# Two transformer blocks on one core: rotary partners from spare weight columns in both mixers, and a top-8 search in the second route

## The chip, the core and the metric

The kernel is written for Trainium2 and runs on one NeuronCore of it. The core has a matrix engine (TensorE, PE in the profile, with its weight loads shown apart as PEld), a vector engine (VectorE, DVE), an activation engine (ScalarE, ACT), GpSimd (POOL) and a queue that issues DMAs (SyncE, SP). Each runs its own list of instructions; they wait for one another through semaphores. The metric is device time in microseconds. The kernel before took 2412.55 us (median of three runs, 2411.41 to 2412.77).

## What is computed

256 tokens of width 1024 pass through a first block of two layers and a second block of one, all in float32. A layer of the first block is a mixer and a feed-forward part: the first layer's is dense, the second layer's is a mixture of 8 experts with 2 chosen per token. The second block is a hybrid layer (a recurrence and a dilated attention), and then a mixture of 32 experts in 4 groups. The parts that matter here, cut from the reference:

```python
def rope(x, positions):                       # in both mixers of the first block
    ...
    x1, x2 = xf[..., :half], xf[..., half:]   # half = 16
    return jnp.concatenate([x1 * cos - x2 * sin, x1 * sin + x2 * cos], axis=-1)

q = (rms_norm(c_q, q_norm_g) @ w_uq).reshape(B, S, MLA_HEADS, MLA_NOPE + MLA_ROPE)   # 8 heads, 64 + 32
q_rope = rope(q[..., MLA_NOPE:], positions)
k_rope = rope(k_r[:, :, None, :], positions)[:, :, 0, :]

# route of the second block's mixture
grp_logits = h @ w_router_group + b_router_group                  # 4 groups
grp = jnp.argmax(grp_logits, axis=-1)
exp_logits = (h @ w_router_expert + b_router_expert).reshape(N, 4, 8)[tok_idx, grp]
top_v, top_i = lax.top_k(exp_logits, 2)
gate = grp_p * jax.nn.softmax(top_v, axis=-1)
```

## The kernel before, in words

**Layout.** Activations lie with channels on the 128 partitions and the 256 tokens in the free dimension (`x_chan`, `h_chan`: 8 tiles of 128x256). Constants of the program lie in one table, `tab_sb` (`TAB`, L47), a 128-row array of 128-column parts such as `ident`, `ones`, `iota` and `rot1`; the queue loads it in the setup between the fourth and the fifth of its weight loads (L363). Weights come from DRAM as a stream of 1 MB slots into a ring of 14 slots, `ring`, by DMAs that SP issues (L138); a slot is loaded again when its user has counted it as used.

**Order of the stages** (L3347 to L3363): setup, mixer 0, dense, mixer 1, first mixture, hybrid, second mixture. Each stage is made of blocks, and every engine waits at the end of a block for the others (the profile shows that as a wait for PEq).

**A mixer's first block** (`stage_mixer`, L546) makes 34 products, listed in `items`: tiles of the input projection (n = 0 to 7), one query product per head (n = 8 to 15, L639), one key product per head, two value products, and eight more tiles of the input projection (n = 26 to 33, L631 and L634). The banks of PSUM go round in fives, and ACT copies each product out. The query product gives 96 rows: 64 plain ones and, on partitions 64 to 95, the 32 that are rotated. The spare part of the weight slot, 32 more columns per head, holds zeros.

**The rotation before.** `turn(i)` (L657) is called on PE behind products 27 to 31. For i < 4 it multiplies the rows 64 to 95 of two heads (32x512) by a 32x32 matrix, `rot1`, that swaps the two halves and negates one; for i = 4 the same for the shared key (32x256). The product goes to one of two PSUM banks (`rot_banks`). DVE waits for it (`rot_done`), multiplies it by the sines (L771), the rows themselves by the cosines (L772) and adds both (L773); for the key L779 to L781. In mixer 0 DVE also computes parts of the modulation vector from side loads of 1 MB (`dve_modulation`, L324), three of them between the rotations. A side load goes out when a slot of its own ring of four is free.

**A mixer's other blocks**: causal attention (L898 and on), and the output projection (L812). At the start of the latter SP begins to load the next stage's weights (`nxt.head`).

**The second route** (`TokenRoute`, L1306) comes before the second mixture. ACT, PE and DVE turn the router's product into 36 logits per token (2 tiles of tokens on 128 partitions). Then DVE works through one instruction after another, each waiting for the one before (`link`): `first_max` (L1292) on the 4 groups; the group's choice is spread over its 8 experts by a product of the choice with itself (L1379); the experts outside the group are pushed down to -1e30 (L1380 to L1382); `first_max` for the best expert with 7 instructions and for the second best with 6; and the sum of both choices (L1385). PE, which has run 10 products only to keep busy (L314), waits for that sum, counts the places (L1350, L1352), DVE makes the selection (L2015), PE gathers the tokens of the first experts (L2047), and the experts' products (L2063, L2086) follow. The ring then has 20 slots, filled before the route ends.

Of the kernel before, what the change touches and what calls it, by code (L numbers as in the profile page):

```python
# [14 lines left out]
P = 128  # L15
# [31 lines left out]
def table_columns():  # L47

    cols = [("ident", 128), ("ones", 128), ("heads2", 128), ("tri", 128), ("rot1", 128), ("rot2", 128),
            ("freq1", 1), ("freq2", 1), ("causal", 128), ("iota", 128), ("eps", 1), ("row", 1)]  # L50
    at, out = 0, {}
    for name, n in cols:
        out[name] = slice(at, at + n)
        at += n
    return out, at
# [490 lines left out]
def stage_mixer(k, l, loads, nxt, norm, nxt_norm, side=None):  # L546
# [4 lines left out]
    with ExitStack() as ctx:  # L551
# [20 lines left out]
        banks, rot_banks, lat_sums = k.bank[1:6], k.bank[6:8], k.bank[0]  # L572
# [11 lines left out]
        rot_done, rope_ready = S("rot_done"), S("rope_ready")  # L584
        forget_step, forget_moved = S("forget_step"), S("forget_moved")
        with nc.Block() as block:
# [31 lines left out]
            def _(pe):  # L618
                def product(n):
# [16 lines left out]
                    elif kind == "query":  # L636
                        w = w.rearrange("p (t h m) -> p t h m", t=2, h=HEADS)
                        for t in range(2):
                            mm = nc.tensor.matmul(b[0:96, 0:T], w[:, t, i, 0:96], cq[:, t, :], start=(t == 0),  # L639
                                                  stop=(t == 1))  # L640
# [16 lines left out]
                def turn(i):  # L657
                    pe.wait_ge(*tile_out.at(10 + 2 * i if i < 4 else 4))
                    if i >= 2:
                        pe.wait_ge(*rope_ready.at(i - 1))  # L660
                    src = qm[64:96, 2 * i:2 * i + 2, :] if i < 4 else misc[64:96, :]
                    nc.tensor.matmul(rot_banks[i % 2][64:96, 0:512 if i < 4 else T], k.t("rot1")[64:96, 64:96], src,
                                     start=True, stop=True).then_inc(*rot_done.up())

                keep_warm(k, k.bank[7], 10 if l else 5)
                for n in range(len(items)):
# [7 lines left out]
                    if 27 <= n < 32:  # L674
                        turn(n - 27)

            @block.scalar
            def _(act):
# [7 lines left out]
                for n, (kind, j, i) in enumerate(items):  # L686
                    act.wait_ge(*item_done(n))
                    b = banks[n % NB]
                    if kind == "query":
                        a(qm[0:96, i, :], b[0:96, 0:T], ACT.Copy, scale=96 ** -0.5).then_inc(*tile_out.up())  # L690
# [31 lines left out]
            def _(dve):  # L722
# [41 lines left out]
                for i in range(5):  # L764
                    dve.wait_ge(*rot_done.at(i + 1))
                    b = rot_banks[i % 2]
                    if i < 4:
                        swapped = b[64:96, :].rearrange("p (h n) -> p h n", h=2)
                        x = qm[64:96, 2 * i:2 * i + 2, :]
                        turned = scratch[64:96, 3:5, :]  # L770
                        link(v.tensor_tensor(turned, swapped, spread(sin[64:96, :], 2), ALU.mult))  # L771
                        link(v.tensor_tensor(x, x, spread(cos[64:96, :], 2), ALU.mult))  # L772
                        v.tensor_tensor(x, x, turned, ALU.add).then_inc(*rope_ready.up())  # L773
                        dve.wait_ge(*rope_ready.last())
# [2807 lines left out]
```

## Time and profile before

| what | us |
|---|---|
| median of three runs | 2412.55 |
| the profiled execution | 2411.62 |
| its span, from the first to the last instruction | 2409.8 |
| setup | 0 to 34.8 |
| mixer 0 | 35 to 181 |
| dense | 181 to 477 |
| mixer 1 | 477 to 628 |
| first mixture and hybrid | 628 to 1952 |
| route of the second mixture | 1952 to 1962 |
| second mixture | 1962 to 2409.8 |

The page of the profile gives PE busy for 92% of the span, DVE for 29%, ACT for 13%, and 734.71 MB moved at a mean of 305 GB/s. Its second part cuts the span into 40 slices and gives for each the busy tenths of every engine, the clock granted to TensorE and the DMA rate; its fourth part follows the chain of work that ended last. From the trace come tables of the instructions in order of time, grouped tables with the mean of one instruction (ns), tables of who waited for whom, and tables of stretches with the busy time of each engine, the granted clock and the DMA rate. In the order-of-time tables a value in brackets is the idle time of the engine before the instruction and what ended it.

### The profile page before, as it was taken

The numbers are of one execution on the slowest core, as the hardware profiler recorded it, in microseconds if no ns is written. First come the engines' busy times: TensorE is split into PE (matmuls) and PEld (weight loads), VectorE is DVE, ScalarE is ACT, GpSimd is POOL, SyncE is SP. The second block draws the span as 40 slices with busy tenths as digits, with TensorE's granted clock in tenths as the row PEclk, the third lists the DMA queues.
The fourth block names the chain that finished last, engine by engine and source line by source line (L and its number), as shares of the span: only waits on it lengthen the run. The fifth ranks groups of instructions, "written<-read, shape, count | busy, mean of one in ns | idle before, by whom it ended". The sixth has DMA issues, their size and how long they took to land. (4 is left out here: it accounts for less than half of the span.)

```text
span 2409.8 us, 47351 instructions
## 1 busy us (share of the span) xinstructions
PE 2223.1 (92%) x21866; PEld 1356.5 (56%) x21866; DVE 689.6 (29%) x1274; ACT 319.3 (13%) x717; POOL 23.2 (1%) x21
## 2 busy tenths in 40 slices
PE   6999999999999999999999999899999997777776
PEld 5778888877734344353534444688789862221221
DVE  6763222336501101101101102455465431111111
ACT  2331000144200000000000000333232110000000
POOL 1000000000000000000000000000000000000000
PEclk9999999999999999999999999999999998877778
DMA  9658555701699999999999999433300579999998
GB/s 398 244 231 336 213 225 209 322 12 60 254 397 407 408 401 419 398 420 401 420 392 420 394 419 417 176 123 140 128 3 4 217 296 421 421 421 422 421 421 365
DMA packets 111472, 734.71 MB, mean 305 GB/s; under 512 B 12768, under 2 KB 16128, under 8 KB 36640
## 3 DMA queue, kind: packets, MB, share of 16 engines
q1 hardware_dynamic: 109328, 724.62, 74.2%
q8 instruction: 176, 2.88, 0.5%
q0 software_dynamic: 1152, 4.19, 0.4%
q10 hardware_dynamic: 784, 2.75, 0.3%
q14 instruction: 32, 0.26, 0.0%
HBM read 721.39 MB, written 10.09 MB: 304 GB/s over the span
## 5 line engine op out<-in xcount | busy, mean ns | idle before, releaser
L1558 PE MATMUL bank<-ring,moe_xg 128*32 128x512 f32 (+1 forms) x6144 | 581.0, 540 | 0.7 <-DVE moe_xg L1714 0.7
L1558 PEld LDWEIGHTS bank<-ring,moe_xg 128*32 128x32 f32 x6144 | 199.1, 110 | 377.3 <-issue 375.3
L1569 PE MATMUL bank<-ring,moe_turned 128*32 128x256 f32 x5376 | 291.5, 379 | 0.0
L1569 PEld LDWEIGHTS bank<-ring,moe_turned 128*32 128x32 f32 x5376 | 174.7, 110 | 117.1 <-issue 3.1
L1117 PE MATMUL bank<-h_chan,ring 128*128 128x256 f32 x896 | 195.6, 379 | 1.4 <-ACT h_chan L503 1.4
L1117 PEld LDWEIGHTS bank<-h_chan,ring 128*128 128x128 f32 x896 | 170.2, 190 | 24.7 <-issue 1.6
L2063 PE MATMUL bank<-ring,late 128*32 128x512 f32 x696 | 122.9, 806 | 51.8 <-DMA ring<-stream 51.8
L1753 DVE TENSOR_TENSOR moe_hidden<-moe_silu,bank 128x512 f32<-128x512 f32 (+1 forms) x48 | 26.9, 617 | 482.9 <-PE bank L1558 482.9
L2508 PE MATMUL bank<-h_chan,ring 128*128 128x256 f32 x672 | 148.0, 380 | 1.9 <-DVE h_chan L2613 1.9
L2508 PEld LDWEIGHTS bank<-h_chan,ring 128*128 128x128 f32 x672 | 127.0, 190 | 23.0 <-issue 6.3
L2063 PEld LDWEIGHTS bank<-ring,late 128*32 128x32 f32 x696 | 17.7, 122 | 150.2 <-DMA ring<-stream 129.8
L1101 PE MATMUL bank<-dense_hidden,ring 128*128 128x256 f32 x448 | 98.8, 379 | 0.0
L1707 DVE COPY moe_y<-bank 32x256 f32<-32x256 f32 x48 | 20.0, 416 | 257.1 <-PE bank L1569 256.5
L1101 PEld LDWEIGHTS bank<-dense_hidden,ring 128*128 128x128 f32 x448 | 85.1, 190 | 11.6
L631 PE MATMUL bank<-h_chan,ring 128*128 128x256 f32 x384 | 85.1, 380 | 1.0 <-ACT h_chan L503 1.0
L2086 PE MATMUL bank<-ring,moe_turned 128*32 128x512 f32 x392 | 58.7, 704 | 27.6 <-DMA ring<-stream 26.8
L631 PEld LDWEIGHTS bank<-h_chan,ring 128*128 128x128 f32 x384 | 72.5, 190 | 15.0 <-issue 5.5
L1615 ACT ACTIVATE moe_silu<-bank 128x512 f32<-128x512 f32 (+1 forms) x48 | 22.6, 544 | 434.6 <-PE bank L1558 434.6
L2129 DVE TENSOR_TENSOR moe_hidden<-late,bank 128x512 f32<-128x512 f32 x8 | 5.5, 687 | 240.2 <-PE bank L2063 240.2
L324 DVE CUSTOM_DVE_ANT_0 ada_product<-ada_slots,ada_c 128x1024 f32<-128x1024 f32 x56 | 68.5, 1223 | 1.5
L1134 DVE TENSOR_TENSOR dense_hidden<-dense_silu,bank 128x512 f32<-128x512 f32 x14 | 9.6, 688 | 201.3 <-PE bank L1117 201.3
L1698 ACT ACTIVATE moe_y<-bank 32x256 f32<-32x256 f32 x48 | 18.1, 377 | 354.2 <-PE bank L1569 353.8
(461 smaller groups left out, 2119.2 us busy)
## 6 DMA issues: line engine op xcount, KB each, us to landing
ring<-stream SPq DMA_DIRECT2D x257, 1024.0 KB, 22.7
ring<-wide SPq DMA_DIRECT2D x240, 1024.0 KB, 16.8
ring<-wide SPq DMA_DIRECT2D x128, 768.0 KB, 16.9
late<-stream SPq DMA_DIRECT2D x47, 1024.0 KB, 27.0
ada_slots<-stream SPq DMA_DIRECT2D x28, 1024.0 KB, 7.2
h_chan<-stream SPq DMA_DIRECT2D x9, 1024.0 KB, 26.7
rows<-zeros SPq DMA_DIRECT2D x8, 512.0 KB
moe_x_rows<-rows SPq DMA_DIRECT2D x28, 96.0 KB, 10.8
```

The source lines that it names most:

```text
L324: mul = k.nc.vector.tensor_tensor_reduce(product, w[:, i * D:(i + 1) * D], c_row, 1.0, 0.0, ALU.mult, ALU.add, accum_out=k.mod[:, l, at:at ...
L631: mm = nc.tensor.matmul(b[:, 0:T], w[:, t, i * P:(i + 1) * P], k.hT[:, t, :], start=(t == 0), stop=(t == DT - 1))
L1101: mm = nc.tensor.matmul(k.bank[t // 2][:, (t % 2) * T:(t % 2) * T + T], w[:, f, t * P:(t + 1) * P], hidden[:, c % 2, f, :], start=(c == 0 ...
L1117: mm = nc.tensor.matmul(b[:, f * T:(f + 1) * T], w[:, t, f * P:(f + 1) * P], k.hT[:, t, :], start=(t == 0), stop=(t == DT - 1))
L1558: mm = self.k.nc.tensor.matmul(banks[r][i * TILE:(i + 1) * TILE, 0:width], self.m.xg[:, r, t * TILE:(t + 1) * TILE], w[:, i, :], start=(t ...
L1569: mm = self.k.nc.tensor.matmul(self.sum_bank[r][q * TILE:(q + 1) * TILE, :], self.m.turned[:, r, n * TILE:(n + 1) * TILE], w[:, f2, q * T: ...
L1615: k.nc.scalar.activation(m.silu[:, r, 0:self.span[c]], self.gate_bank[r][:, 0:self.span[c]], ACT.Silu)\
L1707: last = self.k.nc.vector.tensor_copy(self.m.y[r * TILE:(r + 1) * TILE, q * T:(q + 1) * T], self.sum_bank[r][q * TILE:(q + 1) * TILE, :])
L1753: v.tensor_tensor(m.hidden[:, r, 0:self.span[c]], m.silu[:, r, 0:self.span[c]], self.up_bank[r][:, 0:self.span[c]], ALU.mult).then_inc(*se ...
L2063: mm = k.nc.tensor.matmul((self.gate_bank if j < self.per_proj else self.up_bank)[own, :], m.xg[:, t, own], w[:, i, e, :], start=(t == 0), ...
L2086: mm = k.nc.tensor.matmul(k.bank[half][own, :], m.turned[:, f, own], w[:, i, e, :], start=(f == 0), stop=(f == 3))
L2508: mm = nc.tensor.matmul(b[:, 0:T], lhsT, rhs, start=(t == 0), stop=(t == DT - 1))
```

## The change

It has two parts. In the mixers, the weights' 32 spare columns per query head, and 32 columns of the tile `misc` that holds the shared key, now hold the 32 rotary columns with their halves swapped; so the same product yields the swapped rows on partitions 96 to 127. ACT copies 128 rows instead of 96. The sines on those partitions are taken from a frequency column whose first half is negated. The products with `rot1`, their two semaphores and the table part `rot1` go. DVE takes the swapped rows from SBUF.

In the second route, the mask of the group is added to the logits directly, and both calls of `first_max` on the experts are replaced by `max` (the eight largest values of each row) and `max_index` (their positions), one of each per tile of tokens, a copy that turns positions into float32, and two comparisons with `iota`.

```diff
-    cols = [("ident", 128), ("ones", 128), ("heads2", 128), ("tri", 128), ("rot1", 128), ("rot2", 128),
+    cols = [("ident", 128), ("ones", 128), ("heads2", 128), ("tri", 128), ("rot2", 128),
...
-                            mm = nc.tensor.matmul(b[0:96, 0:T], w[:, t, i, 0:96], cq[:, t, :], start=(t == 0),
-                                                  stop=(t == 1))
+                            mm = nc.tensor.matmul(b[:, 0:T], w[:, t, i, :], cq[:, t, :], start=(t == 0), stop=(t == 1))
...
-                def turn(i):
-                    pe.wait_ge(*tile_out.at(10 + 2 * i if i < 4 else 4))
-                    if i >= 2:
-                        pe.wait_ge(*rope_ready.at(i - 1))
-                    src = qm[64:96, 2 * i:2 * i + 2, :] if i < 4 else misc[64:96, :]
-                    nc.tensor.matmul(rot_banks[i % 2][64:96, 0:512 if i < 4 else T], k.t("rot1")[64:96, 64:96], src,
-                                     start=True, stop=True).then_inc(*rot_done.up())
...
-                    if 27 <= n < 32:
-                        turn(n - 27)
...
-                        a(qm[0:96, i, :], b[0:96, 0:T], ACT.Copy, scale=96 ** -0.5).then_inc(*tile_out.up())
+                        a(qm[:, i, :], b[:, 0:T], ACT.Copy, scale=96 ** -0.5).then_inc(*tile_out.up())
...
-                    dve.wait_ge(*rot_done.at(i + 1))
-                    b = rot_banks[i % 2]
                     if i < 4:
-                        swapped = b[64:96, :].rearrange("p (h n) -> p h n", h=2)
-                        x = qm[64:96, 2 * i:2 * i + 2, :]
+                        dve.wait_ge(*tile_out.at(10 + 2 * i))
+                        swapped, x = (qm[rows, 2 * i:2 * i + 2, :] for rows in (slice(96, 128), slice(64, 96)))
                         turned = scratch[64:96, 3:5, :]
-                        link(v.tensor_tensor(turned, swapped, spread(sin[64:96, :], 2), ALU.mult))
+                        link(v.tensor_tensor(turned, swapped, spread(sin[96:128, :], 2), ALU.mult))
                         link(v.tensor_tensor(x, x, spread(cos[64:96, :], 2), ALU.mult))
-                        v.tensor_tensor(x, x, turned, ALU.add).then_inc(*rope_ready.up())
-                        dve.wait_ge(*rope_ready.last())
+                        link(v.tensor_tensor(x, x, turned, ALU.add))
...
+        link(v.tensor_scalar(col["ghot"], col["ghot"], -NEG, NEG, ALU.mult, ALU.add))
         for tok in range(TT):
-            own = spread_last(m.small["ghot"][:, tok, :], E // G)
-            link(v.tensor_tensor(m.small["hot1"][:, tok, :].rearrange("p (g e) -> p g e", g=G), own, own, ALU.mult))
-        link(v.tensor_tensor(L, L, hot1, ALU.mult))
-        link(v.tensor_scalar(hot1, hot1, -NEG, NEG, ALU.mult, ALU.add))
-        link(v.tensor_tensor(L, L, hot1, ALU.add))
-        first_max(k, m, link, L, E, col["m1"], hot1, col["l2"])
-        first_max(k, m, link, col["l2"], E, col["m2"], hot2, None)
+            own = m.small["l"][:, tok, :].rearrange("p (g e) -> p g e", g=G)
+            link(v.tensor_tensor(own, own, spread_last(m.small["ghot"][:, tok, :], E // G), ALU.add))
+        for tok in range(TT):
+            link(v.max(m.best[:, tok, :], L[:, tok, :]))
+        for tok in range(TT):
+            link(v.max_index(m.best_at[:, tok, :], m.best[:, tok, :], L[:, tok, :]))
+        link(v.tensor_copy(m.best_place[:, :, :], m.best_at[:, :, 0:2]))
+        iota = spread(k.t("iota")[:, 0:E], TT)
+        for i, hot in enumerate((hot1, hot2)):
+            link(v.tensor_tensor(hot, iota, m.best_place[:, :, i:i + 1].broadcast_to([P, TT, E]), ALU.is_equal))
+        col["m1"], col["m2"] = m.best[:, :, 0:1], m.best[:, :, 1:2]
...
+    t[96:128, TAB["freq1"].start] = np.concatenate([-f1, f1])
...
+        misc[:, 96:112], misc[:, 112:128] = kr[:, 16:32], kr[:, 0:16]
...
+        uq[:, :, :, 96:112], uq[:, :, :, 112:128] = uq[:, :, :, 80:96], uq[:, :, :, 64:80]
```

## Rows read from the trace of the kernel before

**Rows 1.** The page: span in 40 slices, in tenths, and GB/s.
```profile
PE   6999999999999999999999999899999997777776
...
PEclk9999999999999999999999999999999998877778
DMA  9658555701699999999999999433300579999998
```
**Rows 2.** Who PE waited for, from 1960 us on: us, times, longest.
```profile
PE bank L2063 <- DMA ring<-stream: 51.8, 60, 2.2
PE bank L2086 <- DMA ring<-stream: 26.8, 26, 1.4
```
**Rows 3.** Stretches: length, PE, PEld, DVE, ACT, POOL busy; clock, DMA share, GB/s.
```profile
180.00:475.00 295.00, 293.28 (x1368) 258.26 (x1369) 86.64 (x148) 17.94 (x32) 0.96 (x1) 1.00 0.64 258
...
655.00:1590.00 935.00, 927.30 (x11789) 421.56 (x11782) 122.97 (x253) 71.15 (x161) 3.79 (x4) 1.00 0.96 384
...
1970.00:2400.00 430.00, 316.28 (x1900) 97.11 (x1892) 57.94 (x105) 7.86 (x16) 0.00 (x0) 0.79 1.01 420
```
**Rows 4.** Order of time, PE, end of mixer 0's first block.
```profile
85.63 1.04 PE L662 MATMUL bank<-qm,tab_sb 32*32 32x512 f32 x2
...
90.25 1.04 PE L662 MATMUL bank<-qm,tab_sb 32*32 32x512 f32 x2
...
104.66 7.17 PE L634 MATMUL bank<-ring,h_chan 128*128 128x256 f32 x32
112.56 0.67 PE L898 MATMUL bank<-km,qm 96*128 96x256 f32 x2 [0.73 <-PEq L586]
```
**Rows 5.** Order of time, DVE, mixer 0.
```profile
83.94 0.08 DVE L324 DVE_READ_ACCUMULATOR2_ANT mod<- 128x1 f32 x1
...
86.81 0.69 DVE L771 TENSOR_TENSOR score<-bank,sin 32x512 f32<-32x512 f32 x1 [2.79 <-PE bank L662]
...
88.97 1.23 DVE L324 CUSTOM_DVE_ANT_0 pT<-ring,score 128x1024 f32<-128x1024 f32 x1
...
91.50 0.69 DVE L771 TENSOR_TENSOR score<-bank,sin 32x512 f32<-32x512 f32 x1
...
104.84 0.42 DVE L779 TENSOR_TENSOR score<-bank,sin 32x256 f32<-32x256 f32 x1 [1.83 <-PE bank L662]
...
108.26 0.17 DVE L344 SCALAR_TENSOR_TENSOR amp<-mod,vec_sb 128x8 f32<-128x8 f32 x1
```
**Rows 6.** Stretches of mixer 0 with the side loads' DMA at the end of each row.
```profile
80.00:85.00 5.00, 5.00 (x25) 4.41 (x24) 3.91 (x8) 0.76 (x2) 0.00 (x0) 1.00 1.01 416
85.00:90.00 5.00, 5.00 (x22) 3.36 (x20) 3.09 (x4) 0.76 (x2) 0.00 (x0) 1.00 0.69 282
```
**Rows 7.** Order of time, mixer 1: PE's first and last rotation, DVE's wait.
```profile
532.16 1.04 PE L662 MATMUL bank<-qm,tab_sb 32*32 32x512 f32 x2
...
533.31 0.69 DVE L771 TENSOR_TENSOR score<-bank,sin 32x512 f32<-32x512 f32 x1 [15.37 <-PE bank L662]
...
551.19 7.17 PE L634 MATMUL bank<-ring,h_chan 128*128 128x256 f32 x32
```
**Rows 8.** Tile `ring`, 60 to 110 us: duration min/median/max in ns, first and last start.
```profile
L631 PEld LDWEIGHTS bank<-h_chan,ring x89: 186/190/190, 59.9 to 94.3; 128*128 128x128 f32 x89
...
L639 PEld LDWEIGHTS bank<-pT,ring x32: 160/163/163, 65.3 to 72.7; 128*96 128x96 f32 x32
```
**Rows 9.** Order of time: twenty of the query's matmuls on PE; copies of 96 and 128 rows.
```profile
49.13 0.40 ACT L698 ACTIVATE pT<-bank 128x256 f32<-128x256 f32 x1
...
65.51 4.48 PE L639 MATMUL bank<-pT,ring 128*96 128x256 f32 x20
...
71.59 0.38 ACT L690 ACTIVATE qm<-bank 96x256 f32<-96x256 f32 x1 [0.17 <-PE bank L639]
```
**Rows 10.** Order of time, setup: DVE's wait for a weight load.
```profile
22.49 1.23 DVE L324 CUSTOM_DVE_ANT_0 h_chan<-ring,h_chan 128x1024 f32<-128x1024 f32 x1 [3.60 <-DMA ring<-stream]
```
**Rows 11.** Order of time, second route: DVE's chain, and PE around it.
```profile
1954.75 0.17 DVE L1298 TENSOR_SCALAR moe_idx<-moe_ghot 128x8 f32<-128x8 f32 x1
...
1954.96 0.17 DVE L1299 TENSOR_TENSOR moe_idx<-moe_idx,tab_sb 128x8 f32<-128x8 f32 x1
...
1955.76 0.42 DVE L1379 TENSOR_TENSOR moe_hot<-moe_ghot 128x32 f32<-128x32 f32 x2
1956.21 0.23 DVE L1380 TENSOR_TENSOR moe_l<-moe_l,moe_hot 128x64 f32<-128x64 f32 x1
...
1956.96 0.22 DVE L1296 TENSOR_REDUCE moe_m<-moe_l 128x2 f32<-128x64 f32 x1
1957.21 0.22 DVE L1297 TENSOR_TENSOR moe_hot<-moe_l,moe_m 128x64 f32<-128x64 f32 x1
...
1960.25 0.23 DVE L1385 TENSOR_TENSOR moe_chosen<-moe_hot 128x64 f32<-128x64 f32 x1
...
1960.53 0.43 PE L1350 MATMUL bank<-moe_chosen,tab_sb 128*128 128x64 f32 x2 [3.23 <-DVE moe_chosen L1385]
```
**Rows 12.** Order of time: both gathers on PE, and SP's first load after the route.
```profile
1962.17 5.44 PE L2047 MATMUL bank<-moe_pick,late 128*128 128x128 f32 x32 [0.56 <-DVE moe_pick L2015]
...
1968.66 6.34 SPq L138 DMA_DIRECT2D ring<-stream  x8
...
1981.68 1.95 PE L2047 MATMUL bank<-moe_pick,late 128*128 128x128 f32 x16
```
**Rows 13.** Stretches around the falls of the clock, second route and mixer 0.
```profile
139.80:143.20 3.40, 3.40 (x18) 2.96 (x14) 1.28 (x4) 0.62 (x2) 0.00 (x0) 0.53 0.00 0
...
1962.20:1965.70 3.50, 3.50 (x17) 3.50 (x18) 0.11 (x1) 0.09 (x1) 0.00 (x0) 0.52 0.00 0
```
**Rows 14.** Order of time, PE in mixer 0's attention, ahead of its fall of the clock.
```profile
138.71 0.66 PE L911 MATMUL bank<-tab_sb,score 128*128 128x128 f32 x4 [1.68 <-DVE score L1004]
...
140.09 2.50 PE L314 MATMUL bank<-tab_sb 128*128 128x128 f32 x10
...
144.94 1.16 PE L314 MATMUL bank<-tab_sb 128*128 128x128 f32 x8
```
**Rows 15.** The chain that ended last: its end and one turn of the stream.
```profile
2373.53 27.82 DMA ring<-stream
...
2401.40 1.11 PE bank L2086 x8
```

More of the change, by code:

```diff
@@ L571, in stage_mixer @@
         z, lo, e, F, negF = (scratch[0:8, i, :] for i in (3, 4, 5, 6, 7))
-        banks, rot_banks, lat_sums = k.bank[1:6], k.bank[6:8], k.bank[0]
+        banks, lat_sums = k.bank[1:6], k.bank[0]
         NB = len(banks)
@@ L583, in stage_mixer @@
         lat_root, lat_ready = S("lat_root"), S("lat_ready")
-        rot_done, rope_ready = S("rot_done"), S("rope_ready")
         forget_step, forget_moved = S("forget_step"), S("forget_moved")
@@ L778, in _ @@
                         turned, own = scratch[64:96, 3, :], scratch[64:96, 4, :]
-                        link(v.tensor_tensor(turned, b[64:96, 0:T], sin[64:96, :], ALU.mult))
+                        link(v.tensor_tensor(turned, misc[96:128, :], sin[96:128, :], ALU.mult))
                         link(v.tensor_tensor(own, misc[64:96, :], cos[64:96, :], ALU.mult))
@@ L2288, in __init__ @@
         self.mark = sb("mark", [1, 8])
+        self.best, self.best_place = sb("best", [P, TT, 8]), sb("best_place", [P, TT, 2])
+        self.best_at = sb("best_at", [P, TT, 8], mybir.dt.uint32)
         self.inverse = sb("inverse", [P, TT])
@@ L3431, in tables @@
     t[:, TAB["tri"]] = (p[:, None] <= p[None, :])
-    rot1 = np.zeros((P, P), np.float32)
-    for i in range(16):
-        rot1[64 + 16 + i, 64 + i] = -1
-        rot1[64 + i, 64 + 16 + i] = 1
-    t[:, TAB["rot1"]] = rot1
     rot2 = np.zeros((P, P), np.float32)
```

## The prediction, made before the changed kernel ran

> **What bounds the kernel now.** I read the page's slices first [rows 1]. PE is at nine tenths until the last eight slices, where it drops to seven and the DMA row stands at nine: the kernel has a long part bound by PE and a last part bound by the weight stream. The stretches say the same [rows 3]: in the dense stage PE is busy for 293.28 of 295 us with the DMA engines at a 0.64 share; in the first mixture 927.30 of 935 us; from 1970 us on PE has 316.28 of 430 us while the DMA moves 420 GB/s without a gap. There PE's waits are for loads [rows 2], and the chain that ended last is DMA to its end [rows 15]. So the reader has to ask two things of an edit: does it shorten what PE does before 1952 us, and does it bring forward the moment at which the last stream restarts? That stream fills its 20 slots before the route ends, stands still, and restarts at 1968.66 when the first slot has been used [rows 12]. From there to the end all is bytes divided by rate. Every stream before it starts at a block's beginning or when PE or DVE gives a slot back; none starts by a time of its own. Hence a stage that ends d earlier moves all behind it by d, whether that part is bound by PE or by DMA.
>
> **Mixers: what goes.** The rotation is five pairs of PE matmuls per mixer between the last products. In mixer 0 the first begins at 85.63 and the last product group, two products long, at 104.66 [rows 4]. That is 19.03 us for four products and five rotations. Two products without a rotation between them take 7.17 us [rows 4], so one takes 3.585, four take 14.34, and the rotations cost 19.03 - 14.34 = **4.69 us** on PE. (One cycle: 90.25 - 85.63 = 4.62, less 3.585, is 1.035 for a 512-wide rotation with its gaps.) Mixer 1 shows 532.16 to 551.19, again 19.03 [rows 7], again 4.69. PE sets the end of the block in both: it waits for nothing until the block's end at 112.56 (0.73 for the others) [rows 4]. Sum: **-9.38 us**.
>
> **What is late next.** In mixer 0 DVE ends at 108.43 and PE at 111.83 [rows 4, 5]. If PE ended at 107.14 and DVE stayed, DVE would keep 1.3 of the 4.69. But DVE too starts earlier: it idled 2.79 us for the first rotation and 1.83 for the last [rows 5], and now needs only the rows of ACT's query copies, which run around 71.6 us [rows 9]. From 83.94 on it has four rotations of 2.16 (86.81 to 88.97), three modulation steps of 2.53 (88.97 to 91.50) and 3.59 for the key and the tail (104.84 to 108.43) [rows 5]: 83.94 + 0.1 + 8.64 + 7.59 + 3.59 = 103.9, which is 3.3 us ahead of PE's new end. The modulation steps need side loads; the DMA falls to a 0.69 share in 85 to 90 us, so its queue is empty at about 88.5 [rows 6], and the last two steps now begin at 90.9 and 95.6. The first would begin at 86.2, with its load three behind the queue's end (2.4 us each at 416 GB/s: 81). Cost: nothing. If that cover were gone, each microsecond of lateness beyond 3.3 would count fully. In mixer 1 DVE waited 15.37 us [rows 7]; all its rotation will be done before PE's last two products start.
>
> **What is added there.** Query weights grow from 96 to 128 columns, which lie in slots that are loaded anyway. A weight load takes 163 ns for 96 columns and 190 for 128 [rows 8]. But twenty query matmuls end in 4.48 us, 0.224 each [rows 9], and products with 128 columns run at the same 3.585/16 = 0.224 [rows 4]: the 256-column stream sets the pace, and the load hides under it. ACT's copy takes 0.38 for 96 rows and 0.40 for 128 [rows 9]. Both at zero; above, 32 loads x 27 ns = 0.86 us per mixer if the load were bare; below zero nothing, since no work goes. The page "TensorE: Matmul & The Clock Gate" of the Trainium skill (Step-by-step: what each phase is for) says that a weight load's time scales with the column count, and the two durations agree with it. Taken as a rule for the time of the products it would speak against this change, and the sum would be 1.7 us higher; the equal pace of the products says it does not reach the path. DVE now multiplies from SBUF instead of PSUM, off the path.
>
> **Setup.** The table shrinks by 128 columns, 65.5 KB. It lies in the queue before the weight load for which DVE waits 3.60 us [rows 10], and DVE sets the setup's end. At 420 GB/s [rows 3] that is **-0.16 us**.
>
> **Second route.** From 1955.76, the first L1379, to 1960.25, the sum of the choices, DVE runs 18 linked instructions in 4.49 us [rows 11], with PE waiting (3.23 us of idle time ends at L1385). All 18 go. In their place, by start-to-start distances: a scalar op on 128x8, 0.21 (1954.75 to 1954.96); two additions on 128x32, 0.45 for both (the two L1379); a copy of 128x4, 0.21 as well; two comparisons on 128x64, 0.26 each, 0.52. That is 1.39. The four search instructions have no row. One takes at least what a tiny op takes, 0.21, and `max` most likely what a reduction on 128x64 takes, 0.25 (1956.96 to 1957.21) [rows 11]. `max_index` reads two inputs and writes eight positions; I bound it by one tiny op below (0.21) and three full ones above (0.76), and take 0.40, in the middle of one and two full ones, since both its inputs are short. So 0.50 + 0.80 = 1.30; bounds 4 x 0.21 = 0.84, and with two full ones for a `max` 2 x 0.51 + 2 x 0.76 = 2.54. New chain 1.39 + 1.30 = 2.69: **-1.80 us** (bounds -2.26 and -0.56). The Trainium skill's "Vector Engine (DVE) Microarchitecture Reference" (The match/index hardware and the swap-based sort pattern) says that finding positions is a separate pass of two instructions, a load of the eight values and a search. By it each `max_index` would be 0.21 + 0.25 = 0.46 and the gain 1.68; no row here shows it.
>
> **The clock behind the route.** PE's granted clock is 0.52 (1.2 GHz for nearly all of it) from 1962.2 to 1965.7 [rows 13], behind the idle 3.23 us and a further 0.56 [rows 11, 12]. The gather of 32 matmuls runs in it and takes 5.44 us, where 16 take 1.95 at full clock [rows 12], 3.90 for 32: the fall costs 1.54. The new wait is 3.23 - 1.80 = 1.43. Nearest rows: in mixer 0 a wait of 1.68 with shorter stops around it is followed by a fall at 139.8 [rows 13, 14], and at 112.56 a stop of 0.73 is not: the slices stay at nine tenths there [rows 1, 4]. 1.43 lies between, nearer the first, but the keep-busy matmuls run right up to it. I take the full clock: **-1.54 us**, the least certain term; bound on the other side 0.
>
> **Sum** against the profiled execution: 2411.62 - 0.16 - 9.38 - 1.80 - 1.54 = 2398.7. The median lay 0.93 above that execution, so **2399.7**.
>
> **Rivals.** (a) The clock still falls behind the shorter wait: 2401.2. For it: 1.68 was enough in the mixer. (b) The search instructions are slow: at 0.78 us each on average (3.10 for the four) the route gains nothing and the clock falls as before, 2403.0. Against: no DVE instruction on so few elements in the chain takes over 0.26. (c) The falls in the mixers' attention move or vanish, as everything behind the first block shifts. There ten keep-busy matmuls took 2.50 us and eight took 1.16 at full clock [rows 14], so about 1.05, and with what follows 1.3 per mixer: 2397.1 with both gone; a new one in another place would cost as much. (d) The mixers' gain is taken back in part by a side load or DVE in mixer 0 that is late by over 3.3 us: up to 4.69 back, 2404.4. (e) Slower: with the table shorter by 512 bytes per partition, every tensor behind it lies at another address. If the stream wrote more slowly there, the last part alone, 432.7 us from 1968.66 to 2401.36 [rows 12, 15], would give back 12.9 us at a rate 3% lower (408 instead of 420 GB/s), and from there on the kernel is slower; at 4% it is 2417. For it speaks only that the last part has no slack at all; against it that very different targets (ring, late, h_chan) now all run at that rate. (f) The change does nothing that shows, because what the rotations cost sits in some wait I misread: 2412.
>
> **Chances.** Forecast 0.46, (a) 0.22, (b) 0.09, (c) 0.11, (d) 0.06, (e) 0.04, (f) 0.02. The range 2396.0 to 2404.5 takes in the forecast, (a), (b), (c), most of (d), and the bounds of the search. A measurement of this kernel can tell about 0.2% (4.8 us) from no change: faster 0.93, same 0.03, slower 0.04.
>
> **What would show it.** Each mixer's last tiles of products would follow one another at 3.585 us without L662, and attention begin 4.85 us earlier in mixer 0 and 9.5 earlier in mixer 1 (both with setup's 0.16). The route from its first instruction to the sum of the choices would be 1.80 shorter, the gather near 3.9 us with a clock of 1.00, and SP's first load after it about 13 us earlier than 1968.66. From there to the end nothing should differ by over a microsecond. I would be wrong if DVE's end replaced PE's in mixer 0, if a search instruction took over 0.5 us, or if the stream's rate moved.

## The result

| | median, us | lowest and highest | runs |
|---|---|---|---|
| before | 2412.66 | 2411.41 to 2412.94 | 4 |
| changed | 2394.76 | 2391.22 to 2396.21 | 4 |

The ratio is 0.9923 [0.9911, 0.9936]: 17.9 us faster, where 12.9 were forecast. The sign was right and the time lies 1.2 us below the range. The profiled execution took 2391.22, the fastest of the four, so its trace shows more gain (20.4 us) than the median does. With the runs of the experiments, before has 51 runs from 2406.6 to 2415.5 with a median of 2411.8, and the changed kernel 15 from 2391.2 to 2396.7 with a median of 2395.0: 16.8 us apart. The first three runs of before lay closer together than the kernel's runs do. Of the ten runs with the rotations put back (ghost_turns), one took 3306.92 us at a granted clock of 0.65 and is left out of what follows.

**The page of the changed kernel**, PE, granted clock and DMA in 40 slices:

```profile
span 2389.4 us, 47297 instructions
...
PE   6999999999999999999999999899999997777776
...
PEclk9999999999999999999999999999999998787777
DMA  9668554802699999999999999343300579999998
```

Against [rows 1] it is the same picture, shorter: a long part at nine tenths of PE, then eight slices in which the DMA row stands high.

**Mixers.** PE in order of time, mixer 0: the last 64 matmuls of one line of products, the 64 of the other, and the first of the attention.

```profile
78.47 13.98 PE L630 MATMUL bank<-h_chan,ring 128*128 128x256 f32 x64
92.29 13.98 PE L633 MATMUL bank<-ring,h_chan 128*128 128x256 f32 x64
106.99 1.32 PE L883 MATMUL bank<-km,qm 96*128 96x256 f32 x5 [0.73 <-PEq L585]
```

The eight products follow one another with nothing between. From 78.47 to 92.29 four take 13.82 us, so 3.455 each. The attention starts at 106.99, against 112.56 in [rows 4]. DVE in the same stretch, its first rotation and its last instruction, and then its first and last step of the rotation in mixer 1:

```profile
83.87 0.69 DVE L757 TENSOR_TENSOR score<-qm,sin 32x512 f32<-32x512 f32 x1
...
103.52 0.17 DVE L344 SCALAR_TENSOR_TENSOR amp<-mod,vec_sb 128x8 f32<-128x8 f32 x1
...
510.80 0.69 DVE L757 TENSOR_TENSOR score<-qm,sin 32x512 f32<-32x512 f32 x1
...
520.33 2.28 DVE L766 TENSOR_TENSOR km<-score 32x2048 f32<-32x2048 f32 x1
```

DVE no longer waits in its rotation ([rows 5] had 2.79 and 1.83) and ends at 103.7, 2.6 us ahead of PE's last product (92.29 + 13.98 = 106.27) and 3.3 ahead of its next block. From SBUF the multiplication takes 0.69, as from PSUM.

**Second route.** DVE from the group's choice to the chosen experts, then PE, then SP's first load:

```profile
1938.41 0.17 DVE L1362 TENSOR_SCALAR moe_ghot<-moe_ghot 128x8 f32<-128x8 f32 x1
...
1939.07 0.42 DVE L1367 MAX8 moe_best<-moe_l 128x8 f32<-128x32 f32 x2
...
1939.53 0.09 DVE L1369 MATCH_VALUE_LOAD moe_best_at<-moe_best,moe_l 128x8 f32 x1
1939.61 0.18 DVE L1369 FIND_INDEX8 moe_best_at<-moe_best,moe_l 128x8 uint32<-128x32 f32 x1
...
1940.12 0.17 DVE L1370 CAST moe_best_place<-moe_best_at 128x4 f32<-128x4 uint32 x1
...
1940.85 0.22 DVE L1375 TENSOR_TENSOR moe_chosen<-moe_hot 128x64 f32<-128x64 f32 x1
...
1941.12 0.43 PE L1335 MATMUL bank<-moe_chosen,tab_sb 128*128 128x64 f32 x2 [1.18 <-DVE moe_chosen L1375]
...
1942.77 3.81 PE L2037 MATMUL bank<-moe_pick,late 128*128 128x128 f32 x32 [0.56 <-DVE moe_pick L2005]
...
1947.63 2.04 SPq L138 DMA_DIRECT2D ring<-stream  x3
```

The four searches, from 1939.07 to the copy at 1940.12, take 1.05 us. PE waits 1.18 instead of 3.23 [rows 11], the gather takes 3.81 instead of 5.44 [rows 12], and the first load goes out at 1947.63 instead of 1968.66, 21.03 earlier. In the three later profiles of the changed kernel it goes out at 1951.69, 1949.69 and 1952.38.

**To the end** the chain is DMA, as in [rows 15]:

```profile
2352.58 27.91 DMA ring<-stream
2380.53 1.11 PE bank L2076 x8
```

From SP's first load to the end of the last DMA it is 432.9 us; it was 432.7. All that was gained by 1947 us arrives at the end, less 0.2 in the stream and 0.5 in the tail.

**The account of the two profiled executions**, from landmarks of the order of time (us). A stage starts with SP's first small load (`posi` for the mixers and the hybrid), attention ends where the output projection's first matmul starts, and the tokens of the first mixture are SP's reads `moe_x_rows` for its first and its last expert.

| stretch | before | changed | difference |
|---|---|---|---|
| mixer 0, start to attention | 77.28 | 71.90 | -5.38 |
| mixer 0, attention | 33.83 | 32.24 | -1.59 |
| mixer 1, start to attention | 79.55 | 74.16 | -5.39 |
| mixer 1, attention | 33.50 | 32.24 | -1.26 |
| mixer 1, output projection to the first tokens of the first mixture | 74.79 | 74.47 | -0.32 |
| last tokens of the first mixture to the hybrid | 224.33 | 221.13 | -3.20 |
| hybrid to the router | 350.82 | 350.81 | -0.01 |
| group's choice to chosen experts | 4.69 | 2.64 | -2.05 |
| first gather | 5.36 | 3.74 | -1.62 |
| last DMA to the end | 8.45 | 8.91 | +0.46 |

The dense stage is 297.7 in both. The mixers' first blocks, the choice and the gather make 14.4 us; attention and the first mixture's end another 6. Is that second part due to the change?

### The profile page after: what moved, and what is told of

It reads as the page before. It is cut to its first block and busy times, and to the rows that moved or that the text cites. A ratio compares the mean times of both kernels' runs of the same rounds, so it can differ in the third digit from the quotient of the medians.

```text
span 2389.4 us, 47297 instructions
## 1 busy us (share of the span) xinstructions
PE 2206.5 (92%) x21846; PEld 1351.1 (57%) x21846; DVE 687.8 (29%) x1268; ACT 319.3 (13%) x717; POOL 23.3 (1%) x21
## 5 line engine op out<-in xcount | busy, mean ns | idle before, releaser
L1086 PEld LDWEIGHTS bank<-dense_hidden,ring 128*128 128x128 f32 x448 | 85.1, 190 | 11.6
L2053 PE MATMUL bank<-late 128*32 128x512 f32 x280 | 47.7, 782 | 21.7 <-DMA late<-stream 21.7
```

The source lines that it names most:

```text
L1086: mm = nc.tensor.matmul(k.bank[t // 2][:, (t % 2) * T:(t % 2) * T + T], w[:, f, t * P:(t + 1) * P], hidden[:, c % 2, f, :], start=(c == 0 ...
L2053: mm = k.nc.tensor.matmul((self.gate_bank if j < self.per_proj else self.up_bank)[own, :], m.xg[:, t, own], w[:, i, e, :], start=(t == 0), ...
```

## Experiments

Three questions. **First**, whether the mixers' 10.8 us are the time of the rotations on PE, or come with what else the change moved (a shorter table, addresses, an earlier DVE). **Second**, whether the gather's clock hangs on the length of the wait ahead of it. **Third**, whether the gain in attention belongs to the change; the theory is that waits of PE bring a lower clock and that filling them gains time, its rival that the falls come and go by themselves and the median doesn't show them. A keep-busy call (`keep_warm`) is one float32 matmul in the program and two in the trace. The kernel before took 2412.0 beside after_again and the kernels with one part alone or before_warm, 2411.6 beside after_look, ghost_turns, slow_route and after_warm2, and 2412.3 beside the rest.

### The same kernel again

No edit. after_again and after_b are five runs each, after_look is one.

> The changed kernel once more, for a profile of another execution. Theory: what does not depend on the clock is fixed at -13.0 us (setup 0.19, two mixer fronts 5.38 and 5.40, route 2.05), and the rest, up to 7.9 us in the first profile, is PE time at the lower clock level, which differs from execution to execution; so the time lies anywhere between 2390 and 2399, and the stage lengths outside stretches of the lower clock repeat within 0.1 us. Rival: everything in the first profile repeats, and the time is 2391 to 2392 each time.

Measured: 2395.17 (2394.49 to 2396.68), 0.9927 [0.9914, 0.9941].

> One more execution of the changed kernel. Both theories: fronts 71.90 and 74.17, route 2.64 from the group's comparison to the sum of the choices, gather 3.8 or 5.4. Theory (the lower clock comes and goes by execution): another set of stretches at 1.2 GHz than in the two profiles so far, and stage lengths that differ only there.

Measured: 2392.8, one run.

> The changed kernel once more, beside the next kernel on the same chip. All theories: 2393 to 2396 median. In 6 of the 7 profiles so far in which the 1.68 us wait was left as it is, each attention took 33.3 to 33.8 us, in the first profile of the changed kernel 32.24; so here too 33.3 to 33.8 in at least one of them.

Measured: 2394.94 (2393.93 to 2395.89), 0.9929 [0.9916, 0.9942]. (after_again's mixer 1, at 32.24, is overlooked in the count of the expectation.)

The first blocks of the mixers, the choice and the gather repeat to 0.01 us in all four profiles (these three and the first). Attention doesn't. In after_again, after_look and after_b it took 33.72, 33.30 and 33.79 in mixer 0 and 32.24, 33.57 and 32.23 in mixer 1. The stretch 132 to 135 us (columns: length, PE, PEld, DVE, ACT, POOL busy; clock, DMA share, GB/s), the changed kernel's first profile and then after_again's:

```profile
132.00:135.00 3.00, 1.85 (x18) 1.52 (x19) 2.41 (x9) 2.54 (x11) 0.00 (x0) 1.00 0.00 0
```

```profile
132.00:135.00 3.00, 2.02 (x12) 1.44 (x12) 2.28 (x7) 2.65 (x11) 0.00 (x0) 0.64 0.00 0
```

PE of the second in order of time:

```profile
132.98 1.12 PE L896 MATMUL bank<-tab_sb,score 128*128 128x128 f32 x4 [1.69 <-DVE score L989]
...
135.07 1.94 PE L314 MATMUL bank<-tab_sb 128*128 128x128 f32 x10
```

Two executions of one program, with the same wait of 1.69, and only one fell. So the 2.85 us in attention are luck of the profiled execution. The end of the first mixture came out at 222.36, 221.12 and 222.41. The 224.33 of before is no fixed cost of the kernel before either: route_only, which has the same mixture and the old mixers, took 220.45.

The lower clock accounts for the differences among these executions. From the first mixer to the end of the gather, the granted clock was at its lower level for 10.2 us in the changed kernel's first profile and for 20.5, 17.1 and 20.5 in the three repeats; in the profile of before it was 23.9. after_again's 10.2 us more cost it 4.2 us from mixer 0's start to SP's first load: 1.5 in mixer 0's attention, 1.5 at the start and 1.2 at the end of the first mixture, with all other rows of the table equal to 0.1.

### One part alone

mixers_only has the change's hunks of the table and of `stage_mixer` with their weights; the route stays as before.

```diff
-                def turn(i):
...
-                        turn(n - 27)
```

> The kernel before with the mixers' part of the change alone. Theory: setup and two fronts, 0.19 + 5.38 + 5.40 = 10.97, and up to 5 us of falls of the clock in the attentions and at the end of the first mixture: 2397 to 2402. The second route keeps its 3.2 us wait and its slow gather of about 5.4 us. Rival (the forecast's own term, 4.69 per mixer, and the rest of the gain sits in the route): 2403 with no more than 9.6 before the second route.

Measured: 2400.39 (2397.57 to 2403.58), 0.9947 [0.9934, 0.9961]: -11.6. The first blocks take 71.90 and 74.17, as in the changed kernel, and the choice 4.69, as before.

```profile
92.44 13.98 PE L633 MATMUL bank<-ring,h_chan 128*128 128x256 f32 x64
107.14 3.69 PE L883 MATMUL bank<-km,qm 96*128 96x256 f32 x16 [0.73 <-PEq L585]
...
1949.77 0.43 PE L1335 MATMUL bank<-moe_chosen,tab_sb 128*128 128x64 f32 x2 [3.24 <-DVE moe_chosen L1370]
1951.41 6.67 PE L2032 MATMUL bank<-moe_pick,late 128*128 128x128 f32 x32 [0.45 <-DVE moe_pick L2000]
```

route_only has the hunks of `TokenRoute.dve` and its tiles; the mixers stay as before.

```diff
-        first_max(k, m, link, L, E, col["m1"], hot1, col["l2"])
-        first_max(k, m, link, col["l2"], E, col["m2"], hot2, None)
...
+            link(v.max(m.best[:, tok, :], L[:, tok, :]))
...
+            link(v.max_index(m.best_at[:, tok, :], m.best[:, tok, :], L[:, tok, :]))
```

> The kernel before with the route's part alone. Theory: the chain from the group's mask to the sum of the choices is 2.05 us shorter, the gather runs at full clock (3.81 instead of 5.44 us) behind a wait of 1.2 us, in all -3.7: 2409.0; if the clock falls behind the shorter wait too, -2.1: 2410.6. All before the route is as before. Rival (the search also pays an entry cost or the route was hidden by the stream): 2412 to 2413.

Measured: 2408.02 (2405.18 to 2413.22), 0.9979 [0.9970, 0.9988]: -4.0. The first blocks take 77.28 and 79.54 and the choice 2.64. The profiled execution was the slowest of the eleven.

```profile
1960.32 0.43 PE L1350 MATMUL bank<-moe_chosen,tab_sb 128*128 128x64 f32 x2 [1.19 <-DVE moe_chosen L1390]
...
1962.09 5.44 PE L2052 MATMUL bank<-moe_pick,late 128*128 128x128 f32 x32 [0.70 <-DVE moe_pick L2020]
```

The parts add up to -15.6, beside -16.8 for the whole; within the intervals nothing says that they touch one another. And here the gather is slow behind a wait of 1.19: the short wait doesn't exclude the fall (rival (a)), it only makes it rarer.

### The rotations put back as empty work

The changed kernel with the table's old length and five matmuls of the old shapes at the old places, whose product nobody reads or waits for:

```diff
+                def turn(i):
+                    src = k.tab[64:96, 0:512 if i < 4 else T]
+                    nc.tensor.matmul(k.bank[6 + i % 2][64:96, 0:512 if i < 4 else T], k.t("ident")[64:96, 64:96], src,
+                                     start=True, stop=True)
...
+                    if 27 <= n < 32:
+                        turn(n - 27)
```

> The changed kernel with the five rotation products of each mixer put back on PE where they stood, on constants of the table, nobody waiting for them; rot1 is back in the table; all else as in the changed kernel. Theory: the products cost PE 5.38 us per mixer by themselves, so the distance from a mixer's first DMA to its attention is 77.28 and 79.55 us again, and the time is some 10.8 above the changed kernel, about 2405 to 2407. Rival: part of the gain came from DVE's waits or from the sines and rows in SBUF; then the distances come out below 77.2 and 79.5.

Measured: 2407.77 (2403.10 to 2410.25, nine runs), 0.9984 [0.9974, 0.9993]. The first blocks take 77.32 and 79.58 us again, as before (77.28 and 79.55), while DVE does its rotation as early as in the changed kernel:

```profile
85.36 1.04 PE L657 MATMUL bank<-tab_sb 32*32 32x512 f32 x2
86.33 3.72 PE L630 MATMUL bank<-h_chan,ring 128*128 128x256 f32 x16
89.98 1.04 PE L657 MATMUL bank<-tab_sb 32*32 32x512 f32 x2
...
112.29 1.97 PE L890 MATMUL bank<-km,qm 96*128 96x256 f32 x8 [0.73 <-PEq L585]
```

```profile
83.74 0.69 DVE L764 TENSOR_TENSOR score<-qm,sin 32x512 f32<-32x512 f32 x1
```

That settles the first question: the mixers' 10.8 us are PE's own time for these five rotations, and DVE's wait took no part. The rows also part the cost of one (two matmuls in the trace): 0.97 from the start of a rotation to the product behind it, and 3.65 from that product to the next rotation, where 16 matmuls among their like take 3.455. So a rotation of 512 columns costs 0.97 for itself and 0.19 around it, and the one of 256 columns 0.54 (104.12 to 104.66 in the profile of before) and the same around it: 4 x 1.16 + 0.73 = 5.4 per mixer, all of the difference. The old addresses came back in this run together with the rotations, so the run alone doesn't part the two. The rows do: the products run at the same distance of 0.216 with the old addresses and with the new.

The median tells less. It lies 12.8 above the changed kernel's 2395.0, where the expectation had 10.8 and 2405 to 2407. These further 2.0 us don't stand in the first blocks.

### The wait ahead of the gather, made long again

The changed kernel with eight linked DVE instructions whose result isn't used, ahead of the new route's `col["m1"], col["m2"]`; timed twice.

```diff
+ for _ in range(8):
+     link(v.tensor_tensor(m.small["idx"][:, :, :], hot1, hot1, ALU.mult))
```

> The changed kernel with eight more linked DVE instructions of 128x64 in the route ahead of the sum of the choices, which PE waits for: 8 x 0.256 = 2.05 us. Theory A (a longer wait of PE brings the lower clock): wait 3.2 us, the gather takes 5.4 instead of 3.8 us, +3.7 in all. Theory B (a wait of 3.2 us and one of 1.2 us differ little, whether the clock falls there is chance): chain +2.05 and the gather 3.8 or 5.4. In both the chain from the group's mask to the sum of choices is 4.69 and nothing before it moves.

Measured: 2400.76 (2398.22 to 2402.50), 0.9957 [0.9942, 0.9972].

> The kernel with eight more linked DVE instructions in the route, again, beside the changed kernel on one chip, since four runs could not tell 3.7 from 5.9 us. Theory A (the longer wait brings the lower clock nearly every time): gather 5.2 to 6.6 us, median 3.5 to 4.0 above the changed kernel's. Theory B (a matter of chance either way): gather 3.8 or 5.4, median 2.0 to 2.9 above.

Measured: 2400.06 (2398.93 to 2402.53), 0.9951 [0.9938, 0.9964], 5.1 above the changed kernel beside it.

```profile
1946.28 2.04 DVE L1375 TENSOR_TENSOR moe_idx<-moe_hot 128x64 f32<-128x64 f32 x8
...
1948.64 0.43 PE L1335 MATMUL bank<-moe_chosen,tab_sb 128*128 128x64 f32 x2 [3.26 <-DVE moe_chosen L1377]
...
1950.28 5.39 PE L2039 MATMUL bank<-moe_pick,late 128*128 128x128 f32 x32 [0.56 <-DVE moe_pick L2007]
```

The delay is 2.07 us, the wait is back at 3.26 and the gather at 5.39: 3.6 us together. Gathers behind a wait of 3.2 were slow in 4 of 4 profiles (before, mixers_only and these two), behind one of 1.2 with the same ten keep-busy matmuls in 1 of 6. So the gather's clock does hang on the wait ahead of it, as theory A has it, with a chance and not a certainty. The median, 5.1 above, lies outside both theories (3.5 to 4.0, and 2.0 to 2.9), and some 1.5 of it stay unexplained. In the profiles one more fall, in mixer 1's attention (33.82 against after_b's 32.23), makes 1.6; whether the other executions had it is not known.

### Filling the waits

On the kernel before: keep-busy matmuls behind the last but one unit of each attention, more of them in the route, and some at the end of the first mixture.

```diff
+ if u == N - 2:
+     keep_warm(k, k.bank[5], 6)          # causal_attention
...
- keep_warm(k, k.bank[5], 10)             # TokenRoute.pe
+ keep_warm(k, k.bank[5], 22)
...
+ keep_warm(k, k.bank[0], 14)             # ahead of the wait for y_ready
```

> The kernel before, unchanged but for keep-busy matmuls on PE in four places where it waited: 6 in each mixer's attention ahead of the 1.68 us wait, 14 ahead of the wait at the end of the first mixture, 22 instead of 10 in the second route ahead of the 3.23 us wait. Theory (the falls follow PE's waits): the falls at 139.8, 586.9, 1528.9 and 1962.2 go, 1.4 + 1.3 + 1.5 + 1.6 = about 5.8 us: 2407. Rival (the falls come from something else, and the matmuls are only added work): 2412.7, or up to 1 us more.

Measured: 2412.14 (2408.55 to 2415.23), 0.9998 [0.9989, 1.0007]. The median did not move, though both attentions took 32.24. The other fillers did not do what they were put there for. First the route, then the end of the first mixture:

```profile
1957.05 5.52 PE L314 MATMUL bank<-tab_sb 128*128 128x128 f32 x44
...
1963.94 3.81 PE L2050 MATMUL bank<-moe_pick,late 128*128 128x128 f32 x32 [0.56 <-DVE moe_pick L2018]
```

```profile
1526.88 5.49 PE L314 MATMUL bank<-tab_sb 128*128 128x128 f32 x28 [4.80 <-issue]
```

In the route the clock fell ahead of the fillers, at 1954.6, where it had not fallen in the profile of before. The 22 calls (44 matmuls) started late and in part at the lower clock (granted 0.91 over 1957.0 to 1962.6). They held the gather at 3.81 but ended past the choice, and cost 0.83 between the choice and the gather. At the end of the mixture the stop of PE, 4.80 us, stands ahead of the 14 calls (28 matmuls) and is no wait for what comes behind them. They could not fill it; the clock fell within it, at 1524.5, and they ran 5.49 us at a granted 0.58. The stretch took 225.84. So this place was not tested. The same on the changed kernel, shorter, and without it:

```diff
+ if u == N - 2:
+     keep_warm(k, k.bank[5], 6)
...
- keep_warm(k, k.bank[5], 10)
+ keep_warm(k, k.bank[5], 14)
```

> The changed kernel with 6 keep-busy matmuls ahead of the 1.68 us wait in both attentions, and 14 instead of 10 in the second route; nothing is added at the end of the first mixture. Theory A (the falls follow PE's waits): both attentions take 32.24 us and the gather 3.8 in every execution, the median falls by 1 to 2 us to about 2393. Theory B (stretches of the lower clock come elsewhere instead): 2394 to 2396, as the changed kernel.

Measured: 2394.81 (2391.21 to 2397.04), 0.9935 [0.9921, 0.9948].

> The changed kernel with 6 keep-busy matmuls in both attentions and 14 in the second route, again, now beside the changed kernel on one chip. Theory A (filling the wait takes the fall away and nothing comes in its place): both attentions 32.2, and the median 2 to 3 us below the changed kernel's beside it. Theory B (what is won there comes back as other stretches of the lower clock): attentions 32.2 all the same, medians within 1 us.

Measured: 2393.85 (2391.72 to 2399.50), 0.9923 [0.9911, 0.9936]. The profile of after_warm2_b around the filled wait of mixer 0, as a stretch and on PE:

```profile
132.00:135.00 3.00, 2.86 (x27) 2.33 (x27) 2.41 (x8) 2.54 (x11) 0.00 (x0) 1.00 0.02 5
```

```profile
131.51 1.60 PE L314 MATMUL bank<-tab_sb 128*128 128x128 f32 x12
...
134.44 1.38 PE L314 MATMUL bank<-tab_sb 128*128 128x128 f32 x10
```

Filled, attention takes 32.2 us in 8 of 8 cases (four profiles, two mixers); unfilled it took 33.3 to 33.8 in 9 of 10 profiles in mixer 0 and in 7 of 10 in mixer 1. So the wait does bring the fall. Yet ten runs of this version have a mean of 2394.6, and the 15 without the filler one of 2394.7. In the profiled execution of after_warm2_b the clock was low twice in the hybrid:

```profile
1532.50:1537.50 5.00, 5.00 (x17) 4.08 (x17) 4.76 (x17) 0.01 (x1) 0.00 (x0) 0.66 0.86 347
...
1809.00:1814.00 5.00, 4.82 (x112) 4.68 (x108) 1.86 (x3) 1.19 (x2) 0.00 (x0) 0.66 0.00 0
```

PE is busy in these stretches, but it had stopped ahead of each:

```profile
1532.02 8.18 PE L2502 MATMUL bank<-h_chan,ring 128*128 128x256 f32 x29 [1.88 <-DVE h_chan L2607]
...
1808.28 1.15 PE L3067 MATMUL bank<-ring,late 64*64 64x64 f32 x32 [1.58 <-DVE ring L3272]
```

The clock fell at 1533.4 and at 1809.9, 1.4 and 1.6 us behind these stops. The stretch from the hybrid to the router took 354.5, and 350.8 in most others. That need not be the price of the filling: route_only's profile, with nothing filled, fell at the same two places (354.4). All 14 profiles have the stop of 1.88 and only three fell behind it, two of the four filled ones and one of the ten others. With eight more calls at the end of the first mixture:

```diff
+ keep_warm(k, k.bank[0], 8)              # ahead of the wait for y_ready
```

> As after_warm2_b, and 8 keep-busy matmuls (2.0 us at full clock, 3.9 at the lower) ahead of the wait of 3.8 us at the end of the first mixture. Theory A: the distance from the last read of the first mixture's rows to the hybrid stage is 220.4 to 221.2 us, as in the profiles with the shortest one, 1 to 2 us below the usual; median 1 us below after_warm2_b. Theory B: the lower clock there does not come from that wait, the distance stays between 221 and 223.

Measured: 2396.29 (2391.89 to 2401.35), 0.9935 [0.9921, 0.9948]. The end of the mixture took 223.72, longer than in the changed kernel's four profiles (221.12 to 222.41), and a low stretch stands in the hybrid again. Here too the stop stands ahead of the fillers:

```profile
1514.11 3.79 PE L314 MATMUL bank<-tab_sb 128*128 128x128 f32 x16 [3.37 <-issue]
```

No version came out clearly ahead of the changed kernel. So the third question has two answers. The waits in attention bring the falls there (16 of 20 unfilled, 0 of 8 filled), as the theory says; that filling them shortens the median is not shown.

## Why the forecast was right, and where it was not

**What bounds the kernel**: right. A stage that ends earlier moved all behind it; the last stream kept its length (432.5 to 432.9 us in all 14 profiles), so rival (e) fell with its price of 12.9 us.

**Mixers, what goes**: the mechanism was right, the term was too small. Forecast 4.69 per mixer, measured 5.38, with 1.39 missed in the sum. The step that failed is "Two products without a rotation between them take 7.17 us [rows 4], so one takes 3.585". The 7.17 runs to the end of the last matmul, which the next one overlaps (a matmul lasts 0.379 in the profile and the next starts 0.216 after it), and these two products stand behind a rotation, where the second matmul starts 0.320 after the first; from start to start two products among their like take 6.91. With 3.455 the same subtraction gives 19.03 - 13.82 = 5.21. The rest lies at both ends: from the start of these products to the first rotation it was 7.00 (78.63 to 85.63) where two now take 6.91, and from the last two products' start to the attention 7.90 where it is 7.79. The Trainium skill, "TensorE: Matmul & The Clock Gate" (Single matmul latency; Back-to-back issue gap), gives a single matmul a constant on top of its columns that the distance between two doesn't have. Of the 0.26 us between 7.17 and 6.91, 0.16 are such an end, which agrees in kind, though the ends of matmuls are modelled in these profiles and prove little; the other 0.10 come from the rotation.

**What is late next**: right. DVE's end was forecast at 103.9 and came at 103.7; rival (d) did not happen.

**What is added**: right at zero. Twenty query matmuls take 4.48 us with 96 columns [rows 9] and with 128, though their loads grew from 163 to 190 ns:

```profile
65.32 4.48 PE L638 MATMUL bank<-pT,ring 128*128 128x256 f32 x20
```

**Setup**: not to be told. Mixer 0 starts at 34.6 to 35.5 us in all profiles of both tables, and -0.16 is lost in that.

**Second route**: forecast -1.80, measured -2.05, inside the bounds. What was too dear was `max_index`, at 0.40. The rows of L1367 and L1369 (ns: lowest, median, highest):

```profile
L1367 DVE MAX8 moe_best<-moe_l x2: 194/194/195, 1939.1 to 1939.3; 128x8 f32<-128x32 f32 x2
L1369 DVE MATCH_VALUE_LOAD moe_best_at<-moe_best,moe_l x2: 92/92/92, 1939.5 to 1939.8; 128x8 f32 x2
L1369 DVE FIND_INDEX8 moe_best_at<-moe_best,moe_l x2: 184/184/185, 1939.6 to 1939.9; 128x8 uint32<-128x32 f32 x2
```

`max_index` is two instructions, and both together take 0.30 from start to start. The Trainium skill's "Vector Engine (DVE) Microarchitecture Reference" (The match/index hardware and the swap-based sort pattern) is borne out by these rows as to the two instructions. The 0.46 that the forecast worked out from it was too high, since the load costs 0.09 and not what a small arithmetic instruction costs; the step that failed was to take 0.21 as the least that an instruction can take. [rows 5] already had a DVE instruction of 0.08.

**The gather**: forecast -1.54, measured -1.62, with rival (a) seen in 1 of 6 profiles instead of the 0.22 it was given.

**Rivals (b) and (f)** are out: no search takes over 0.2 us, and the rotations' cost sat where it was read. **Rival (c)**, the falls in attention: forecast as luck of a new place, at 1.3 each. The first profile shows both gone, 2.85 us, and the repeats show that it is luck of an execution. Whether the kernel has a part in how often is open: with the rotations on PE both attentions fell in all three unfilled profiles (6 of 6 cases), without them in 10 of 14, too few to tell from chance.

**The sum**: 10.77 + 2.05 + 1.62 = 14.4 us are tied to the change by experiments; 12.7 had been counted for them. The medians differ by 16.8. About 2.4 us are left, and ghost_turns has 2.0 of the same kind. In the profiles such differences lie where executions of one program differ among themselves (attention, start and end of the first mixture, at times the hybrid and the tail), by the time at the lower clock; what decides how often the clock falls there, and so the cause of the 2.4 us, stays open.

**Why the time left the range.** The mis-sized terms alone don't do it: 2412.55 - 14.4 = 2398.1 lies inside. The term that was put at nothing is the clock's change from one execution to the next. Rival (c) counted it for the two attentions only, and as an effect of the shift; "The median lay 0.93 above that execution, so **2399.7**" starts from three runs within 1.4 us, and the range holds the bounds of single terms and nothing for such a change, though the forecast itself gives a measurement 4.8 us of doubt. The runs show 2406.6 to 2415.5 for before, with 2411.8 in the middle, and profiles of one program from 10.2 to 20.5 us at the lower clock, which makes 4.2 us. That the changed kernel's median fell outside on the fast side rests on these about 3 us.

## What to carry to other kernels

Cost a removed matmul by start-to-start distances on both sides of the removal, never by the length of a row, which includes the end of its last matmul. A foreign matmul in a stream costs its own distance and a little around it, here 0.97 and 0.19. When a profile shows more gain than its parts explain, profile the same kernel again before giving the rest a cause: here 10.2 us more at the lower clock made one execution 4.2 us longer up to the last stream. On rows of 32 values `max` and `max_index` turned a chain of eighteen linked DVE instructions into one of ten (twelve in the trace), 2 us shorter, and the clock behind it gave 1.6 us more, in five of six profiles. Before a filler is put in, the trace has to show that the stop stands behind its place and not ahead of it.

## What the hardware showed beyond the forecast

- `MATCH_VALUE_LOAD` takes 0.092 us, where arithmetic on 128x8 takes 0.17; `MAX8` and `FIND_INDEX8` on 128x32 float32 take 0.194 and 0.184.
- A stop of 1.69 us was followed by the lower clock in 9 of 10 profiles at one place, one of 1.2 in 1 of 6 at another, one of 3.2 in 4 of 4. The length of the stop alone doesn't decide it: one of 1.88 in the hybrid was followed by a fall in 3 of 14 profiles, one of 1.77 in none. And at the start of the first mixture the clock fell in all 14, though PE had stopped for only 0.42 us in the 7 us ahead. In the changed kernel's first profile, PE in order of time and two stretches:

```profile
629.31 7.93 PE L1524 MATMUL bank<-moe_pick,moe_h_tok 128*128 128x96 f32 x32 [0.42 <-PEq L1158]
```

```profile
629.31:633.70 4.39, 4.39 (x19) 4.39 (x19) 2.05 (x13) 1.28 (x1) 1.74 (x2) 1.00 0.09 36
633.70:637.80 4.10, 3.54 (x15) 3.30 (x14) 0.75 (x3) 0.00 (x0) 2.26 (x3) 0.50 0.90 367
```

- Keep-busy matmuls slow down with the clock: 28 took 5.49 us (0.196 each) in part at the lower clock, 10 took 1.38 (0.138 each) at the full clock. A filler sized at the full clock can overrun the wait that it was to fill, as the 22 calls in the route did.
